# A depthwise convolution on TensorE: 31 taps over 128 channels, or 9 lags over 4 time phases x 32 channels

## The chip, the cores and the metric

The kernel runs on all 8 cores of one Trainium2 chip. Every core runs the same program on one of the 8 sequences of the batch; the cores exchange nothing. The metric is the device time in microseconds (us) of the slowest core.

## The reference

Two layers over x of shape (8, 2048, 1024). What a layer computes:

```python
h = rmsnorm(x, g_mix)
zq, zf, zi, zog, zglu, zga, zgb = split(h @ w_in)
o = hgrn2_recurrence(silu(zq), 1 - f, zi, log f)        # 4 heads of 128, chunked gated linear recurrence
y_a = (rmsnorm(o) * silu(zog)) @ w_br_a
u = (zglu[:, :512] + b) * sigmoid(zglu[:, 512:] + b)    # GLU, 512 channels
u = causal_dwconv(u, conv_w, conv_b)                    # 31 taps, each channel by itself
y_b = silu(layernorm(u)) @ w_br_b                       # LayerNorm over the 512 channels
x = x + (sigmoid(zga) * y_a + sigmoid(zgb) * y_b) @ w_out
x = x + conv_ffn(rmsnorm(x)); x = x + sigmoid(rmsnorm(x) @ w_ple_gate) * (p @ w_ple_proj)
```

The change touches only the branch with `u`: the GLU's output, the depthwise convolution, the LayerNorm behind it, and the order of the work that surrounds them.

## The kernel before, in words

Channels lie on partitions and time along the free dimension. A sequence is worked in two halves of T = 1024 frames (`hf`), so `mixer` (L468) is called four times: two layers, two halves. One call goes through these stages, each of them a list of instructions in a fixed order for each engine; there is no scheduler on the chip, and an engine takes its instructions in order. Every operation goes through one of the helpers `mm` (L266), `act` (L275), `tt` (L279), `stt` (L283), `ts` (L288 or L291), `cp` (L295), so the profile's lines are those of the helpers; waits on semaphores come from the tiles that an operation reads and writes.

- Gates: projections for q, f, v and the output gate (`gate_ph1`, `gate_ph2`). They end in Ln and Exp on ScalarE and a scan on VectorE.
- `fill_steps` (L569), a generator, and `rec_steps` (L627), another, are woven into one another (L694 to L702). `fill_steps` first makes the GLU: for each of 4 blocks of 128 channels and each of 2 time tiles of 512, 8 matmuls for the gate half and 8 for the value half, a sigmoid, and a `stt` into `u[cc]`. Then comes the convolution: for each block `cc` and time tile, 31 matmuls of 512 columns accumulate in one PSUM bank; tap k's stationary matrix is 128x128 with the tap's 128 weights on its diagonal, its moving operand is `u[cc]` shifted by k. The 124 diagonal matrices are made by VectorE for every call (`build_dg`, L565: identity times a column of weights). An activation adds the bias and writes `uc32[cc]` in float32. That makes 48 steps, 16 of the GLU and 32 of the convolution.
- `rec_steps` is the recurrence over 8 chunks of 128 frames in 34 steps: `keys` (4 transposes, 8 score matmuls, masks), `outer` (4 matmuls, the state's update on VectorE, its copy on ScalarE), `rows` (8 matmuls, a square, a product), `scale` (1 matmul with ones, Ln, Exp, a product). Banks 0 to 4 of PSUM belong to it, one for each kind of result; banks 5 to 7 to `fill_steps`. After step i of `fill_steps`, the steps of the recurrence are emitted until `done * 48 >= (i + 1) * 34`.
- LayerNorm (L705 to L737): casts and squares of `uc32` by time tile, 16 matmuls with a matrix of ones that sum over the channels, then for each time tile mean and variance, Ln, Exp, and for each block subtract, multiply, Silu into `ucs[cc]`.
- Branches (L739 to L776): for each of 8 output blocks, 16 matmuls for gate A (`pA`), 8 for branch A (`pC`), a sigmoid and a product, then 16 for gate B (`pB`) and 8 for branch B (`pD`, which read `ucs`), a sigmoid, a product and a sum into `y[oc]`. `ps2()` hands out four pairs of PSUM banks in turn.
- The output projection, woven with the next norm.

Weights come in blocks of up to 1 MB through five SBUF slots: `wrel` frees a block and issues the next load on the POOL queue (`w_emit_upto`). The SP queue loads x at the start and stores the output at the end, and is idle in between.

Of the kernel before, what the change touches and what calls it, by code (L numbers as in the profile page):

```python
# [18 lines left out]
NCOL = 368  # L19
C_GMIX, C_GFFN, C_GPLE, C_GFIN, C_HGN, C_BGLU, C_CW, C_CB, C_LNG, C_LNB, C_FW, C_FB, C_LG0, C_LG1 = (  # L20
    0, 8, 16, 24, 32, 33, 41, 165, 169, 173, 177, 309, 353, 357)
NCONST = 128 + 128 + 512
# [1010 lines left out]
```

How the kernel before makes its waits and increments, by code:

```python
    def _wait(self, eng, deps):  # L70
        for k, v in deps.items():
            if self.seen[eng].get(k, 0) >= v:
                continue
            self.seen[eng][k] = v
            sem = self.sem[k] if isinstance(k, str) else k
            self.q[eng].append(lambda e, sem=sem, v=v: e.wait_ge(sem, v))
# [22 lines left out]
    def op(self, eng, fn, reads=(), writes=(), inc=True):  # L99
        self._wait(eng, self._deps(eng, reads, writes))
        if inc:
            self.cnt[eng] += 1
            c = self.cnt[eng]
            sem = self.sem[eng]
            self.q[eng].append(lambda e, fn=fn, sem=sem: fn(e).then_inc(sem, 1))
        else:
            c = self.cnt[eng] + 1
            self.q[eng].append(fn)
        for t in _flat(reads):
            if t.r.get(eng, 0) < c:
                t.r[eng] = c
        for t in _flat(writes):
            t.w = (eng, c)
            t.r = {}
# [1 line left out]
    def dma(self, eng, fn, out_t=None, in_t=None, sem_t=None):  # L116
        reads = [in_t] if in_t is not None else []
        writes = [out_t] if out_t is not None else []
        self._wait(eng, self._deps(eng, reads, writes))
        st = out_t if out_t is not None else sem_t
        if st.dsem is None:
            st.dsem = self.new_sem()
        st.dcnt += 16
        sem, v = st.dsem, st.dcnt
        self.q[eng].append(lambda e, fn=fn, sem=sem: fn(e).then_inc(sem, 16))
        if out_t is not None:
            out_t.w = (sem, v)
            out_t.r = {}
        if in_t is not None:
            in_t.r[sem] = v
```

## Time and profile before

| | |
|---|---|
| runs, us | 2771.02, 2443.6, 2827.24 (median 2771.02) |
| the profiled execution | 2442.08 us; span of its slowest core 2440.5 us |
| spans of the 8 cores | 2420.8 to 2440.5 us, mean granted TensorE clock 0.969 to 0.975 |
| PE busy | 2246.7 us (92%), 10528 matmuls |
| VectorE (DVE) busy | 1436.5 us (59%), 2357 instructions |
| ScalarE (ACT) busy | 1125.6 us (46%), 1442 instructions |
| DMA queue of POOL (q0), of SP (q1) | 140.55 MB and 39.3%, 17.49 MB and 2.4% of 16 engines' span |

The profile is one execution, on the slowest core. Its parts are the busy times, the span in 40 slices, the DMA queues, the chain of waits that ended last, the costliest groups of instructions, and the DMA issues. A PE that shows as busy is not at its peak, because the durations of pipelined matmuls overlap: the distance from one start to the next is what a matmul costs.

### The profile page before, as it was taken

How to read it: one execution, taken by the hardware profiler on the slowest of the kernel's cores; microseconds unless marked ns; L12 is line 12 of the kernel's file. 1: busy time of each engine (PE TensorE's matmuls, PEld its weight loads, DVE VectorE, ACT ScalarE, POOL GpSimd, SP SyncE). 2: the span in 40 equal slices, each digit the busy share in tenths (PEclk: the TensorE clock that was granted, in tenths of full speed). 3: DMA queues.
4: the chain of work that ended last, by engine and by line, in shares of the span. 5: the costliest groups of instructions: out<-in, count | busy, mean ns of one | idle time of the engine just before them, and what ended most of it. 6: DMA issues, size and time to landing. Idle time of an engine off the chain costs nothing.

```text
span 2440.5 us, 30096 instructions; the slowest of 8 cores (2420.8 to 2440.5 us)
## 1 busy us (share of the span) xinstructions
PE 2246.7 (92%) x10528; PEld 1018.0 (42%) x10528; DVE 1436.5 (59%) x2357; ACT 1125.6 (46%) x1442; POOL 146.8 (6%) x169
## 2 busy tenths in 40 slices
PE   3898898988999999999888989989899999999985
PEld 1344343443444444444334433445334444444432
DVE  3665356753589538943666553666437982697256
ACT  2644235442277507752445343453425771576144
POOL 0000000000000100010000000000000010001000
PEclk9999999999999999999999999989999999999998
DMA  9430352403443555364434206242064454546533
GB/s 199 85 57 1 52 76 42 74 1 52 70 77 56 67 86 86 47 89 73 63 50 71 34 9 95 35 70 35 9 95 69 61 68 67 90 63 84 75 48 138
DMA packets 175523, 159.96 MB, mean 66 GB/s; under 512 B 3856, under 2 KB 166032, under 8 KB 175376
## 3 DMA queue, kind: packets, MB, share of 16 engines
q0 software_dynamic: 165584, 140.55, 39.3%
q1 hardware_dynamic: 9792, 17.49, 2.4%
q8 instruction: 87, 1.43, 0.2%
q14 instruction: 60, 0.49, 0.1%
HBM read 290.18 MB, written 8.39 MB: 122 GB/s over the span
## 4 chain that ended last, share of the span: by engine, by line
PE 81%; DVE 8%; ACT 4%; DMA 4%; issue 3%; SPq 1%; DVEq 0%; another core or an unknown queue 0%; ACTq 0%; POOLq 0%
PE ps L266 80%; DVE arena L279 4%; ACT arena L275 3%; DVE arena L283 2%; DMA ws_sb<-w_br_b 1%; DMA ws_sb<-w_br_a 1%; ACT L275 1%; DMA x_sb<-xT 1%; SPq L386 1%; DMA outT<-arena 1%; DVE h_sb L283 0%; DVE arena L528 0%; DVE x_sb L279 0%; PE ps L634 0%; DVE arena L288 0%
## 5 line engine op out<-in xcount | busy, mean ns | idle before, releaser
L266 PE MATMUL ps<-h_sb,ws_sb 128*128 128x512 bf16 x5376 | 1219.4, 386 | 61.3 <-DVE arena L283 24.1
L266 PEld LDWEIGHTS ps<-h_sb,ws_sb 128*128 128x128 bf16 x5376 | 529.3, 99 | 713.8 <-issue 109.1
L275 ACT ACTIVATE arena<-ps 128x1024 bf16<-128x1024 f32 (+4 forms) x500 | 405.4, 830 | 737.9 <-PE ps L266 735.9
L266 PE MATMUL ps<-arena,ws_sb 128*128 128x512 bf16 x2816 | 649.3, 388 | 56.1 <-DVE arena L279 32.5
L283 DVE SCALAR_TENSOR_TENSOR arena<-arena,cv_sb 128x1024 f32<-128x1024 bf16 x352 | 432.4, 1280 | 43.0 <-ACT arena L275 41.5
L266 PEld LDWEIGHTS ps<-arena,ws_sb 128*128 128x128 bf16 x2816 | 278.5, 99 | 409.2 <-issue 93.7
L279 DVE TENSOR_TENSOR arena<-arena 128x1024 bf16<-128x1024 f32 (+2 forms) x288 | 257.0, 910 | 109.5 <-ACT arena L275 103.6
L266 PE MATMUL ps<-arena 128*128 128x512 bf16 (+3 forms) x1632 | 285.6, 315 | 12.0 <-ACT arena L275 8.5
L279 DVE TENSOR_TENSOR arena<-arena,ps 128x1024 f32<-128x1024 f32 x96 | 116.8, 1220 | 282.1 <-PE ps L266 219.6
L275 ACT ACTIVATE arena<-arena 128x512 f32<-128x512 f32 (+2 forms) x308 | 223.0, 747 | 121.6 <-DVE arena L279 78.6
L275 ACT ACTIVATE arena<-ps,cv_sb 128x1024 f32<-128x1024 f32 (+1 forms) x240 | 255.0, 1062 | 37.5 <-PE ps L266 33.5
L279 DVE TENSOR_TENSOR x_sb<-ps,x_sb 128x1024 f32<-128x1024 f32 x64 | 78.3, 1224 | 282.7 <-PE ps L266 282.7
L266 PEld LDWEIGHTS ps<-arena 128*128 128x128 bf16 (+1 forms) x1632 | 144.6, 98 | 145.2 <-issue 15.3
L275 ACT ACT_TABLE_LOAD x96 | 123.2, 1283 | 161.0 <-PE ps L266 142.5
L275 ACT ACTIVATE arena<-x_sb 128x512 bf16<-128x512 f32 x216 | 115.8, 617 | 114.9 <-PE ps L266 76.0
L266 PE MATMUL ps<-arena,ones 128*128 128x512 bf16 x320 | 89.5, 394 | 46.6 <-ACT arena L275 21.1
L283 DVE SCALAR_TENSOR_TENSOR h_sb<-x_sb,cv_sb,arena 128x512 bf16<-128x512 f32 x160 | 109.0, 746 | 0.0
L288 DVE TENSOR_SCALAR arena<-ident,cv_sb 128x128 bf16<-128x128 bf16 x496 | 85.3, 253 | 3.5 <-PE ps L266 3.5
L283 DVE SCALAR_TENSOR_TENSOR arena<-ps,cv_sb,arena 128x512 f32<-128x512 f32 (+1 forms) x64 | 47.7, 745 | 57.0 <-ACT arena L275 45.6
L327 POOL DMA_DIRECT2D ws_sb<-w_up x48 | 42.0, 876 | 618.4 <-PE ps L266 618.4
L266 PEld LDWEIGHTS ps<-arena,ones 128*128 128x128 bf16 x320 | 31.6, 99 | 96.2 <-issue 66.1
L327 POOL DMA_DIRECT2D ws_sb<-w_in x40 | 35.1, 882 | 555.8 <-PE ps L266 553.6
(49 smaller groups left out, 583.5 us busy)
## 6 DMA issues: line engine op xcount, KB each, us to landing
ws_sb<-w_in POOLq DMA_DIRECT2D x40, 1024.0 KB, 13.5
ws_sb<-w_up POOLq DMA_DIRECT2D x40, 1024.0 KB, 10.2
ws_sb<-w_down POOLq DMA_DIRECT2D x32, 704.0 KB, 7.4
x_sb<-xT SPq DMA_DIRECT2D x32, 256.0 KB, 16.6
ws_sb<-w_out POOLq DMA_DIRECT2D x8, 1024.0 KB, 14.4
ws_sb<-w_ple_gate POOLq DMA_DIRECT2D x8, 1024.0 KB, 10.2
outT<-arena SPq DMA_DIRECT2D x32, 256.0 KB, 2.3
ws_sb<-w_br_a POOLq DMA_DIRECT2D x8, 512.0 KB, 12.7
```

The source lines that it names most:

```text
L266: P.op("pe", lambda e: e.matmul(out_ap, l_ap, r_ap, start=start, stop=stop), reads=[l_t, r_t], writes=[out_t], inc=inc)
L275: P.op("act", lambda e: e.activation(out=out_ap, in_=in_ap, func=func, **kw), reads=[in_t] + list(rd), writes=[out_t])
L279: P.op(eng, lambda e: e.tensor_tensor(out=out_ap, in0=a_ap, in1=b_ap, op=op), reads=[a_t, b_t], writes=[out_t])
L283: P.op("dve", lambda e: e.scalar_tensor_tensor(out=out_ap, in0=a_ap, scalar=scalar, in1=b_ap, op0=op0, op1=op1), reads=[a_t, b_t] + list(r ...
L288: P.op(eng, lambda e: e.tensor_scalar(out=out_ap, in0=a_ap, scalar1=s1, scalar2=None, op0=op0), reads=[a_t] + list(rd), writes=[out_t])
L327: return e.dma_start(out=sap[:, 0:k * ncol].rearrange("p (k n) -> p k n", k=k), in_=src[l, :, c0:c0 + ncol].rearrange("(k p) n -> p k n", ...
L386: P.dma("sp", lambda e, kc=kc: e.dma_start(out=xt[kc][hf][t_].ap, in_=xT[kc * 128:(kc + 1) * 128, c0:c0 + 512]), out_t=xt[kc][hf][t_])
```

## The change

The convolution is laid out anew. T = 1024 frames are split into 4 phases (frame t = 4 tau + f) of 256 frames each, and a tile holds 4 phases x 32 channels on its 128 partitions: there are 16 such groups (`NG`) in place of 4 blocks of 128 channels. Output phase b at tau is a sum over input phases a and lags m = 0 to 8 with weight w[30 - (4m + b - a)], so a group takes 9 matmuls of 256 columns, whose 128x128 stationary matrices have four times four blocks of 32x32, each diagonal. VectorE builds the 9 matrices of a group in one product of broadcast operands (`build_dg(g)`), from a table that the host lays out (`cwv`). Four groups' matrices are kept (`NDG`).

- The GLU's `stt` writes `us[cc % 2]` phase by phase (a permuted write); then 16 DMAs on the SP queue (`to_phases`), each 32 partitions x 256 frames in bfloat16, move it to `uP[cc]`. Two `us` tiles take turns.
- Each group's output gets its bias in an activation of 256 columns.
- The sums of the LayerNorm move into `fill_steps` as four steps of their own, 8 matmuls of 256 columns each, with a block matrix of ones (`ones4`) that sums the 32 channels of each phase.
- `ln_apply(cc)`: subtract and multiply over 1024 columns, four Silu of 256 columns, and 16 DMAs on the SP queue that move the result to 128 channels on partitions, with time still ordered by phase; branch B's last product reads PSUM in permuted order.
- The weave has 28 steps in place of 48, and the recurrence starts after the fourth (`lead`).
- Branches, first half: `ln_apply` and branch A in turn for `oi` = 0 to 3, then branch B for `oi` = 0 to 3; second half: A and B in turn. Each `ln_apply(oi)` is emitted ahead of branch A's sigmoid.
- At the start, four small loads more on the POOL queue.

```diff
+    def dmas(self, eng, fns, out_t, in_t):
+        self._wait(eng, self._deps(eng, [in_t], [out_t]))
...
+        for fn in fns:
+            out_t.dcnt += 16
+            self.q[eng].append(lambda e, fn=fn, sem=sem: fn(e).then_inc(sem, 16))
...
-            def build_dg(tiles, cc, part):
-                for k in range(part * 8, min(part * 8 + 8, 31)):
-                    ts(tiles[k], tiles[k].ap, ident, ident.ap, cvl.ap[:, C_CW + cc * 31 + k:C_CW + cc * 31 + k + 1], None, ALU.mult, rd=[cvl])
+            def build_dg(g):
+                d = dgP[g % NDG]
+                tt(d, d.ap.rearrange("p (m c) -> p m c", c=32), i32, i32.ap.unsqueeze(1).to_broadcast([128, NLAG * PH, 32]),
+                   cwv[l], cwv[l].ap[:, g, :].unsqueeze(2).to_broadcast([128, NLAG * PH, 32]), ALU.mult)
+
+            def to_phases(cc):
+                s_ = us[cc % 2].ap.rearrange("p (f t) -> p f t", f=PH)
+                fns = []
+                for q_ in range(4):
+                    for f_ in range(PH):
+                        fns.append(lambda e, q_=q_, f_=f_: e.dma_start(out=uPv[cc][32 * f_:32 * f_ + 32, q_, HALO:UW],
+                                                                      in_=s_[32 * q_:32 * q_ + 32, f_, :]))
+                P.dmas("sp", fns, uP[cc], us[cc % 2])
...
+                        stt(us[cc % 2], usv[:, :, t_ * 128:(t_ + 1) * 128].rearrange("p f t -> p t f"),
+                            pa, pa.ap.rearrange("p (t f) -> p t f", f=PH), cvl.ap[:, C_BGLU + cc:C_BGLU + cc + 1],
+                            sg, sg.ap.rearrange("p (t f) -> p t f", f=PH), ALU.add, ALU.mult, rd=[cvl])
                         if cc >= 2:
-                            build_dg(dg[0][1], 0, (cc - 2) * 2 + t_)
+                            build_dg((cc - 2) * 2 + t_)
                         yield
+                    to_phases(cc)
...
-                        for k in range(31):
-                            tk = dg[cc % 2][1][k]
-                            mm(pc, pc.ap, tk, tk.ap, u[cc], u[cc].ap[:, t_ * 512 + k:t_ * 512 + k + 512], k == 0, k == 30, k == 30)
+                for g2 in range(NG // 2):
...
+                        for m in range(NLAG):
+                            mm(pc, pc.ap[:, j * TAU:(j + 1) * TAU], d, d.ap[:, m * 128:(m + 1) * 128],
+                               uP[cc], uPv[cc][:, q_, HALO - m:HALO - m + TAU], m == 0, m == NLAG - 1, m == NLAG - 1)
+                        act(uc32[cc], uc32[cc].ap[:, q_ * TAU:(q_ + 1) * TAU], pc, pc.ap[:, j * TAU:(j + 1) * TAU], AF.Identity,
+                            bias=cvl.ap[:, C_CB + g:C_CB + g + 1], rd=[cvl])
+                        if g + NDG < NG:
+                            build_dg(g + NDG)
...
+                    for src_, dst_ in ((ucb[cc % 2], p1), (sqb[cc % 2], p2)):
+                        for q_ in range(4):
+                            mm(dst_, dst_.ap[:, 0:TAU], ones4, ones4.ap, src_, src_.ap[:, q_ * TAU:(q_ + 1) * TAU],
+                               cc == 0 and q_ == 0, cc == 3 and q_ == 3, q_ == 3)
...
             n_side = 34
-            n_main = 48
+            n_main = 28
+            lead = 4
             done = 0
             for i, _ in enumerate(fill_steps()):
-                while done * n_main < (i + 1) * n_side:
+                while done * (n_main - lead) < (i + 1 - lead) * n_side:
...
+            def ln_apply(cc):
+                mt, vt = lnst["mt"], lnst["vt"]
+                v3 = uc32[cc].ap.rearrange("p (q t) -> p q t", q=4)
+                tt(uc32[cc], v3, uc32[cc], v3, mt, mt.ap.unsqueeze(1).to_broadcast([128, 4, TAU]), ALU.subtract)
+                tt(uc32[cc], v3, uc32[cc], v3, vt, vt.ap.unsqueeze(1).to_broadcast([128, 4, TAU]), ALU.mult)
+                for q_ in range(4):
+                    g = 4 * cc + q_
+                    act(un[cc], un[cc].ap[:, q_ * TAU:(q_ + 1) * TAU], uc32[cc], v3[:, q_, :], AF.Silu,
+                        bias=cvl.ap[:, C_LNB + g:C_LNB + g + 1], scale=cvl.ap[:, C_LNG + g:C_LNG + g + 1], rd=[cvl])
...
+                P.dmas("sp", fns, ucs[cc], un[cc])
...
+            y = [None] * 8
+            for oi in range(4):
+                ln_apply(oi)
+                branch_a(0, oi)
+            for oi in range(4):
+                branch_b(0, oi)
...
+            for oi in range(4):
+                branch_a(1, oi)
+                branch_b(1, oi)
```

## Rows read from the trace of the kernel before

**Rows 1.** The page's chain of waits that ended last: shares by engine.

```profile
PE 81%; DVE 8%; ACT 4%; DMA 4%; issue 3%; SPq 1%; DVEq 0%; another core or an unknown queue 0%; ACTq 0%; POOLq 0%
```

**Rows 2.** Windows: from the GLU's start to the LayerNorm's sums, all four calls.

Columns: the stretch and its length, then for each engine the busy time and its instructions, then the granted clock, the DMA engines' share and GB/s.

```profile
107.10:227.90 120.80, 109.34 (x592) 54.03 (x593) 72.35 (x222) 53.07 (x86) 3.25 (x4) 0.94 0.34 49
416.50:533.30 116.80, 107.57 (x592) 53.15 (x592) 72.27 (x218) 53.01 (x86) 3.25 (x4) 0.94 0.36 53
1292.00:1408.70 116.70, 105.61 (x592) 52.84 (x593) 72.35 (x222) 52.95 (x86) 3.25 (x4) 0.97 0.34 53
1597.70:1714.50 116.80, 107.56 (x594) 53.26 (x594) 72.27 (x218) 53.05 (x86) 3.25 (x4) 0.94 0.33 52
```

**Rows 3.** Windows of the second call: GLU, convolution, sums, first output block.

```profile
416.50:463.30 46.80, 39.73 (x214) 19.71 (x214) 28.96 (x65) 25.45 (x40) 1.49 (x2) 0.85 0.59 85
463.30:529.30 66.00, 63.88 (x363) 31.96 (x363) 41.14 (x149) 23.56 (x40) 1.76 (x2) 1.00 0.22 33
529.30:533.30 4.00, 3.97 (x16) 1.48 (x16) 2.17 (x7) 4.00 (x8) 0.00 (x0) 1.00 0.01 2
533.30:555.50 22.20, 13.27 (x49) 4.93 (x49) 13.10 (x20) 15.68 (x20) 0.00 (x0) 0.84 0.00 1
```

**Rows 4.** Timeline of PE, second call, in the GLU.

Columns: start, length in us, engine, line, operation, count, and in brackets the idle time before it and what ended it.

```profile
423.08 3.57 PE L266 MATMUL ps<-h_sb,ws_sb 128*128 128x512 bf16 x8 [6.59 <-ACT hsm L275]
...
446.97 0.39 PE L634 MATMUL ps<-ident,arena 128*128 128x128 bf16 x4
447.19 1.19 PE L266 MATMUL ps<-arena 128*128 128x64 bf16 x8
448.31 1.90 PE L266 MATMUL ps<-h_sb,ws_sb 128*128 128x512 bf16 x8
450.05 0.61 PE L266 MATMUL ps<-arena 128*128 128x128 bf16 x8
450.50 3.62 PE L266 MATMUL ps<-h_sb,ws_sb 128*128 128x512 bf16 x16
453.95 0.39 PE L266 MATMUL ps<-arena 128*128 128x128 bf16 x4
```

**Rows 5.** Groups of instructions by form: busy us, mean ns.

```profile
L266 PE MATMUL ps<-arena 128*128 128x512 bf16 x992 | 228.4, 379 | 3.5 <-DVE arena L283 3.5
...
L275 ACT ACTIVATE arena<-ps 128x1024 f32<-128x1024 f32 x96 | 97.8, 1023 | 329.5 <-PE ps L266 329.3
...
L288 DVE TENSOR_SCALAR arena<-ident,cv_sb 128x128 bf16<-128x128 bf16 x496 | 85.3, 253 | 3.5 <-PE ps L266 3.5
...
L279 DVE TENSOR_TENSOR arena<-arena 128x512 f32<-128x512 f32 x72 | 47.6, 688 | 29.3 <-ACT arena L275 26.8
...
L343 POOL DMA_DIRECT2D ws_sb<-w_down x32 | 34.1, 1067 | 325.5 <-PE ps L266 325.5
...
L275 ACT ACTIVATE arena<-arena,cv_sb 128x512 bf16<-128x512 f32 x32 | 25.2, 810 | 4.8 <-DVE arena L279 4.7
...
L279 DVE TENSOR_TENSOR arena<-ps,mask 128x256 bf16<-128x256 f32 x32 | 13.4, 418 | 7.0 <-PE ps L266 7.0
...
L295 DVE CAST arena<-arena 128x512 bf16<-128x512 f32 x32 | 11.1, 421 | 0.0
```

**Rows 6.** Timeline of ACT, second call: the LayerNorm's Silu of the first time tile.

```profile
537.31 1.28 ACT L275 ACT_TABLE_LOAD   x1 [0.87 <-DVE arena L279]
538.61 2.33 ACT L275 ACTIVATE arena<-arena,cv_sb 128x512 bf16<-128x512 f32 x3
```

**Rows 7.** The SP queue's stores of the output: issue, and time to landing.

```profile
L946 SPq DMA_DIRECT2D outT<-arena x32: 332/332/344, 2397.6 to 2438.1; - x32
...
DMA to landing us min/median/max: 2.2/2.3/4.1
```

**Rows 8.** The SP queue's loads of x, beside weight loads.

```profile
L386 SPq DMA_DIRECT2D x_sb<-xT x32: 328/684/4388, 2.9 to 59.6; - x32
...
DMA to landing us min/median/max: 7.3/16.6/23.1
```

More of the change, by code:

```diff
@@ L18 @@
 DFF = 2816
[L19 to L22, printed above, removed]
+PH = 4
+NG = 16
+NLAG = 9
+TAU = T // PH
+HALO = NLAG - 1
+NCOL = 280
+C_GMIX, C_GFFN, C_GPLE, C_GFIN, C_HGN, C_BGLU, C_CB, C_LNG, C_LNB, C_FW, C_FB, C_LG0, C_LG1 = (
+    0, 8, 16, 24, 32, 33, 41, 57, 73, 89, 221, 265, 269)
+NCONST = 128 + 128 + 512 + 32 + 128
 ARENA = 77824
@@ L214, in build_nc @@
         uhalo = Tl(uhalo_sb[:], "uhalo")
+        cwv = [Tl(cwv_sb[:, l], "cwv%d" % l) for l in range(DEPTH)]
+        i32 = Tl(i32_sb[:], "i32")
+        ones4 = Tl(ones4_sb[:], "ones4")
         stash = Tl(stash_sb[:], "stash")
@@ L624, in mixer @@
+                mt, vt = AR(75008, 1024, F32, "mt"), AR(76032, 1024, F32, "vt")
+                act(mt, mt.ap, p1, p1.ap[:, 0:TAU], AF.Identity, scale=1.0 / 512)
+                tt(vt, vt.ap, mt, mt.ap, mt, mt.ap, ALU.mult)
+                stt(vt, vt.ap, p2, p2.ap[:, 0:TAU], 1.0 / 512, vt, vt.ap, ALU.mult, ALU.subtract)
+                act(vt, vt.ap, vt, vt.ap, AF.Ln, bias=EPS)
+                act(vt, vt.ap, vt, vt.ap, AF.Exp, scale=-0.5)
+                lnst["mt"], lnst["vt"] = mt, vt
             p_tr, p_sc, p_kv, p_o, p_ss = bank1[0:5]
@@ L724, in mixer @@
-            for t_ in range(2):
-                sl = slice(t_ * 512, (t_ + 1) * 512)
-                p1, p2 = lnp[t_]
-                mt, vt = mt2[t_], vt2[t_]
-                act(mt, mt.ap, p1, p1.ap, AF.Identity, scale=1.0 / 512)
-                tt(vt, vt.ap, mt, mt.ap, mt, mt.ap, ALU.mult)
-                stt(vt, vt.ap, p2, p2.ap, 1.0 / 512, vt, vt.ap, ALU.mult, ALU.subtract)
-                act(vt, vt.ap, vt, vt.ap, AF.Ln, bias=EPS)
-                act(vt, vt.ap, vt, vt.ap, AF.Exp, scale=-0.5)
-                for cc in range(4):
-                    tt(uc32[cc], uc32[cc].ap[:, sl], uc32[cc], uc32[cc].ap[:, sl], mt, mt.ap, ALU.subtract)
-                    tt(uc32[cc], uc32[cc].ap[:, sl], uc32[cc], uc32[cc].ap[:, sl], vt, vt.ap, ALU.mult)
-                    act(ucs[cc], ucs[cc].ap[:, sl], uc32[cc], uc32[cc].ap[:, sl], AF.Silu,
-                        bias=cvl.ap[:, C_LNB + cc:C_LNB + cc + 1], scale=cvl.ap[:, C_LNG + cc:C_LNG + cc + 1], rd=[cvl])
@@ L995, in _cvec, with _cwv @@
     return cv
+def _cwv(inp):
+    w = np.asarray(inp["conv_w"], np.float32)
+    out = np.zeros((DEPTH, PH, 32, NG, NLAG, PH), np.float32)
+    for m in range(NLAG):
+        for a in range(PH):
+            for b in range(PH):
+                d = PH * m + b - a
+                if 0 <= d <= 30:
+                    out[:, a, :, :, m, b] = w[:, 30 - d, :].reshape(DEPTH, NG, 32).transpose(0, 2, 1)
+    return out.reshape(DEPTH, 128, NG * NLAG * PH)
 def _consts():
@@ L1005, in _consts @@
     c[:, 256:768] = sm
+    c[:, 768:800] = np.tile(np.eye(32, dtype=np.float32), (PH, 1))
+    c[:, 800:928] = np.kron(np.eye(PH, dtype=np.float32), np.ones((32, 32), np.float32))
     return c
```

208 lines of the change are left out of this document (108 added, 100 removed).

## The prediction, written before the result was known

> **What bounds the kernel now.** I read the chain of waits first: TensorE holds 81% of it [rows 1], so an edit is worth what it does to TensorE's time, once that time isn't replaced by waits. Then I took the windows between the GLU's start and the LayerNorm's sums, for all four calls of `mixer` [rows 2]: 120.8, 116.8, 116.7 and 116.8 us, with VectorE busy for only 72 of them. The split of the second call [rows 3] shows three different stretches. In the GLU (46.8 us) TensorE waits and runs at a clock of 0.85. In the convolution (66.0 us) it is busy for 63.9 us at full clock, with 363 matmuls: nothing but TensorE bounds it. In the first output block (22.2 us) it has 48 matmuls, 10.4 us of work, and waits 12 us for the LayerNorm.
>
> Unit costs come from distances between starts [rows 4]: 8 matmuls of 512 columns take 450.05 - 448.31 = 1.74 us, so 0.216 us each. Eight of 128 columns take 0.45 us, 0.056 each. The 256-column matmul of the change isn't in the trace; by these two it takes 0.108. A chunk of the recurrence costs TensorE 0.22 + 1.12 (`keys`) + 0.45 (`rows`) + about 0.22 (`outer`, four of 128 columns) + 0.22 (`scale`) = 2.2 us. On VectorE it costs five operations of 0.69 and two masks of 0.42 [rows 5], 4.3 us.
>
> **GLU stretch.** Its 256 matmuls take 16 x 1.73 = 27.6 us as before. The opening wait of 6.5 us for `glub` and the cold start behind it (8 matmuls in 3.57 us, not 1.74) stay [rows 4]: the slot is freed and filled as before; I keep 3.5 us for the cold clock. With `lead` the recurrence starts at the fifth step and makes 17 steps (by the weave's condition) by the end, not 11: five `keys`, five `outer`, four `rows`, three `scale`, 10.3 us. ScalarE gets tight, with five operations of 0.6 us a chunk, two table loads of 1.28 around each Ln (the load: [rows 6]) and 1.4 sigmoids of 0.7, 6.5 us against TensorE's 7.1. I add 4 us of waits. Sum 6.5 + 27.6 + 3.5 + 10.3 + 4 = 51.9 us, against 46.8.
>
> The permuted `stt` has as many elements as before; no row shows a permuted write. Its bounds are none and twice 0.75 us, 6 us a call on VectorE, which has 17 us idle here [rows 3]; I take none. `to_phases` adds 16 DMAs a tile on SP, which is otherwise idle. An issue takes 0.332 us and a landing 2.3 [rows 7]: 5.3 + 2.3 = 7.6 us. Behind a tile's DMAs waits the `stt` that writes the same `us` two blocks later, some 13 us on (a block is 6.9 us of GLU plus about 3 of recurrence). So it is covered, and by twice the issue price just so. The fourth tile is read only after 12 groups.
>
> **Convolution and sums.** TensorE now needs 144 x 0.108 = 15.6 us, was 248 x 0.216 = 53.6. Here the bound moves to VectorE. A build is 1152 elements with two tensor operands; from 256 to 512 columns a `tensor_tensor` grows from 418 to 688 ns [rows 5], 1.05 ns an element, so a build takes 0.418 + 896 x 0.00105 = 1.36 us alone and about 1.23 in a row. The bound below is a rate twice that, 0.65 us, which the bfloat16 builds of before suggest (253 ns for 128 elements, 85.3/496 = 0.172 in a row). I take 1.23, since the nearest rows in kind are those of `tensor_tensor`. The first six steps of the convolution carry 12 builds (14.8 us) and nine recurrence steps (9.1 us): 23.9 us of VectorE against 108 x 0.108 + 4.7 = 16.4 us of TensorE. With 1.6 us of waits inside the recurrence and 2 us for the last two steps, whose builds are done by then, the convolution takes 27.5 us. Then the four LayerNorm steps: ScalarE has four squares of 1.05, two Ln-Exp pairs, a copy and a square, 7.8 us, and the state's update goes ahead of the first cast, so 9.5 us. Sum 37 us, against 66 + 4 = 70.0 [rows 3].
>
> Casts, halo copies and bias activations are hidden: the same columns, and 8 more fixed costs of 0.2 us on a ScalarE that isn't the bound there. That cover goes only if ScalarE were full.
>
> The Trainium skill, VectorE: DVE Perf Modes, Mode 2x_1P, wants 16-bit elements with a step of one in both operands for two results a cycle. The weight operand here has step zero, so by that page the build stays at the slow rate; no row here shows a product of two bfloat16 tensors, and the sum would be the same.
>
> So from GLU to sums 88.9 us, was 116.8: 27.9 us less in three calls. The first call's opening wait is 4.3 us, not 6.5 (the same view of TensorE), so 86.7 against 120.8, 34.1 less. Together 117.8 us less.
>
> **LayerNorm and first output block.** Here it pays back. The engines' orders couple three things: VectorE takes subtract, multiply (1.22 each), then `t1s`, which waits for the sigmoid; ScalarE takes a table load 1.28, four Silu of 256 columns (0.81 for 512 [rows 5], so about 0.56 each in a row), another load 1.28, the sigmoid 1.02; the next `ln_apply` starts behind `t1s`. One round is 2.44 + 1.28 + 2.24 + 1.28 + 1.02 + 1.22 + 0.2 = 9.7 us, where TensorE's branch A has 24 x 0.216 = 5.2. From the last recurrence matmul, statistics and the first multiply take 5.6 us, the first Silu set 3.5 more, three rounds 29: the last `un` is whole at 38 us. Its 16 DMAs end 7.6 us later, at 45.7. No weight load runs then (DMA share 0.00 [rows 3]). Only now can the first `pD` run: 1.7 us, plus 3.4 for a cold clock after a wait of over 10 us, 50.8. By then TensorE has 120 matmuls behind it. Before, that point was at 22.2 + 72 x 0.216 = 37.8. So 13 us more a call, 52 in all. The wait for `br1` in the second half (issued after the same release) and what follows don't change. The four start-up loads, 0.7 us of POOL issue each, go behind the first four blocks: nothing.
>
> **Sum.** -117.8 + 52 = -66, against the profiled execution's 2442.08: **2376 us**. The median of the three runs shown is 2771, 13% above it, the lowest 2443.6: the forecast is for an execution like the profiled one.
>
> **Rivals.**
>
> The DMAs decide (slower). The Trainium skill, DMA: Bandwidth & Descriptors, Rules for kernel authors, says that transfers under 64 KB are mostly overhead and should be joined; these are 16 KB. In rows: SP's loads of x took 0.684 us at the median and landed after 16.6 beside weight loads [rows 8], and POOL's costliest issue is 1.07 [rows 5]. At 0.684 the queue falls behind in the first output block, 9.1 + 64 x 0.684 + 2.3 = 55.2 against 45.7: +38 us, 2414. At 1.07 it ends at 79.9, +34 a call, and in the GLU each tile takes 17 us, so that `us` and the last blocks wait some 20 more: +54 x 4, 2592, slower. It turns at 0.8 us an issue, where the two extras make 17 us a call. For it: nothing in the trace moves 32 partitions. Against: 32 stores went at 0.332 without exception. By the fixed 2.0 us of that page's Anatomy of one DMA, taken one after another, it would be slower still.
>
> The recurrence has a floor of its own (no change). Now chunks go by every 12 us, hidden by matmuls. My forecast wants 7 to 9. Transpose, copy, scores, mask, rows, square, Ln, Exp and product are each a hop between engines; if a chunk can't go under 10 us, GLU to sums stays at 101 instead of 88.9: +48, 2424. For it: PE waits for ScalarE at the first chunks. Against: VectorE and ScalarE have 18 and 21 us idle in the GLU [rows 3].
>
> Cheap builds (faster). At 0.65 us TensorE bounds the convolution again, 7 us less a call: 2348.
>
> The gain isn't there at all: if a 256-column matmul cost 0.14 us (what the 64-column ones cost, 1.12/8 [rows 4]), TensorE would need 4.6 us a call more, mostly under VectorE: +8. That stays inside the range.
>
> **Chances.** Forecast 0.52, cheap builds 0.10, recurrence floor 0.25, DMA 0.13 (0.10 of it beyond 2491). Two per cent, 49 us, is what a measurement of this kernel tells from no change: 2393 and 2491. Of the forecast's own case 0.04 lies above 2393. Faster 0.48 + 0.10 = 0.58, same 0.04 + 0.25 + 0.03 = 0.32, slower 0.10. The range goes from 2335 (cheap builds and 3 us less waiting a call) to 2440 (the floor, with some of the DMA's price).
>
> **What would show it.** Right: conv matmuls at 0.108; builds near 1.3 us; GLU to sums 85 to 93 us with VectorE over 80% busy in the convolution; eight table loads in each first half of the branches; TensorE waiting over 8 us ahead of the first `pD`, released by a DMA into `ucs`; SP issues of 0.33. Wrong: `stt` of the GLU waiting for the SP queue, chunks at a pace over 9 us, or a first output half no longer than before.

## The result: 5% slower

The kernel after the change takes 2571.56 us (median of four executions, 2564.91 to 2661.25), against 2607.31 for the four of the kernel before that were run beside it (2442.49 to 2827.24). The ratio is 1.052, 95% interval 1.046 to 1.058: slower. (In some executions of every kernel one die runs at a lower clock and ends later; the ratios leave these out, and where e3 is spoken of as 2467 us, that is the longest span of its undisturbed die.) The profiled execution took 2564.91 us, its span 2563.4, against 2442.08 and 2440.5. The forecast was 2376.

The page of the kernel after: busy time by engine, then the chain of waits that ended last.

```profile
PE 2183.7 (85%) x10176; PEld 1019.1 (40%) x10176; DVE 1480.4 (58%) x1869; ACT 1168.5 (46%) x1502; POOL 148.9 (6%) x173
...
PEclk9977899868999999999998689987789999999998
...
PE 68%; DVE 12%; ACT 9%; issue 6%; SPq 2%; DMA 2%; DVEq 0%; ACTq 0%; another core or an unknown queue 0%
```

TensorE has 63 us less to do and its share of the chain falls from 81% [rows 1] to 68%; VectorE, ScalarE and the issue of instructions take its place. The clock row has sixes and sevens where the mixer's four calls lie. The windows say where the time went: GLU's start to the end of the sums, all four calls, the columns as in [rows 2].

```profile
108.00:244.19 136.19, 90.52 (x505) 53.02 (x505) 85.34 (x109) 56.40 (x89) 3.25 (x4) 0.74 0.37 53
444.90:579.89 134.99, 88.22 (x505) 52.16 (x505) 85.17 (x105) 56.63 (x90) 3.25 (x4) 0.75 0.35 54
1348.90:1487.75 138.85, 93.35 (x505) 54.19 (x505) 85.33 (x109) 56.38 (x89) 3.25 (x4) 0.72 0.34 51
1688.10:1826.91 138.81, 93.19 (x505) 54.39 (x505) 85.33 (x105) 56.65 (x90) 3.25 (x4) 0.71 0.34 51
```

These are 548.8 us, where [rows 2] add up to 471.1: +77.7, forecast -117.8. The rest of the span is 45.2 us longer (122.9 in all), forecast +52. So nearly the whole error lies in this stretch. Split as in [rows 3], second call:

```profile
444.90:508.60 63.70, 45.66 (x244) 22.75 (x243) 46.44 (x60) 32.08 (x49) 1.49 (x2) 0.84 0.50 76
508.60:562.70 54.10, 33.75 (x222) 23.65 (x219) 32.84 (x37) 18.86 (x36) 1.75 (x2) 0.72 0.30 45
562.70:579.89 17.19, 8.80 (x42) 5.76 (x43) 5.89 (x9) 5.69 (x8) 0.00 (x0) 0.55 0.00 0
579.89:634.09 54.20, 31.27 (x121) 12.50 (x120) 15.77 (x15) 27.21 (x34) 1.49 (x2) 0.81 0.22 39
```

GLU 63.7 (forecast 51.9), convolution 54.1 (27.5), sums 17.2 (9.5). The last row is A0 to A3 with B0, 54.2 (50.8). No engine is full in any of them, so this is a matter of waits. TensorE's timeline, second call (columns as in [rows 4]):

```profile
485.42 0.38 PE L290 MATMUL ps<-arena 128*128 128x128 bf16 x4 [2.66 <-ACT arena L299]
485.63 3.25 PE L290 MATMUL ps<-h_sb,ws_sb 128*128 128x512 bf16 x8
...
508.38 1.47 PE L290 MATMUL ps<-arena 128*128 128x128 bf16 x13
518.46 2.08 PE L290 MATMUL ps<-arena 128*128 128x256 bf16 x9 [8.61 <-ACT arena L299]
...
538.28 2.08 PE L290 MATMUL ps<-arena 128*128 128x256 bf16 x9 [4.67 <-ACT arena L299]
...
552.75 1.15 PE L290 MATMUL ps<-arena 128*128 128x256 bf16 x9 [2.62 <-ACT arena L299]
...
565.78 2.29 PE L290 MATMUL ps<-arena,ones 128*128 128x256 bf16 x9 [3.47 <-DVE arena L319]
...
621.92 0.38 PE L290 MATMUL ps<-arena,ws_sb 128*128 128x512 bf16 x1 [3.58 <-DMA arena<-arena]
632.01 2.29 PE L290 MATMUL ps<-arena,ws_sb 128*128 128x512 bf16 x5 [9.71 <-DMA arena<-arena]
```

Nine matmuls of a group take 1.15 us at full clock, the next start 0.98 later, 0.109 each as forecast (552.75). Behind the waits of 8.61 and 4.67 us they take 2.08, at the lower of the clock's two levels (granted 0.50 in both stretches). The wait of 8.61 us stands in front of the second group of a pair. What it waited for, on ScalarE and on VectorE:

```profile
510.02 0.59 ACT L299 ACTIVATE arena<-ps 128x512 bf16<-128x512 f32 x1
517.33 0.63 ACT L299 ACTIVATE arena<-arena 128x512 bf16<-128x512 f32 x1 [6.71 <-DVE arena L303]
517.86 0.46 ACT L299 ACTIVATE arena<-ps,cv_sb 128x256 f32<-128x256 f32 x1
```

```profile
510.71 3.15 DVE L307 SCALAR_TENSOR_TENSOR arena<-ps,cv_sb,arena 128x512 f32<-128x512 f32 x2 [1.39 <-ACT arena L299]
513.47 1.57 DVE L303 TENSOR_TENSOR arena<-i,cwv_sb 128x1152 bf16<-128x1152 bf16 x1
514.96 0.68 DVE L303 TENSOR_TENSOR arena<-ps,S 128x512 f32<-128x512 f32 x1
515.74 1.49 DVE L303 TENSOR_TENSOR arena<-arena,hsm 128x512 f32<-128x512 f32 x2
```

All waits of 0.7 to 8.6 us in this convolution stand ahead of the second group of a pair. The two groups share one PSUM bank, which is one tile to the kernel's dependency tracking. The second group writes that tile, so it must wait until the bias activation of the first has read it; that activation (517.86) stands behind the recurrence's copy (517.33), and the copy behind VectorE's queue of products and a build.

By form, the changed instructions:

```profile
L307 DVE SCALAR_TENSOR_TENSOR arena<-ps,cv_sb,arena 128x512 bf16<-128x512 f32 x32 | 79.6, 2489 | 8.3 <-PE ps L290 4.1 <-ACT arena L299 3.8
L303 DVE TENSOR_TENSOR arena<-i,cwv_sb 128x1152 bf16<-128x1152 bf16 x64 | 90.2, 1409 | 34.0 <-PE ps L290 34.0
L290 PE MATMUL ps<-arena 128*128 128x256 bf16 x576 | 112.8, 365 | 79.9 <-ACT arena L299 79.9
L299 ACT ACT_TABLE_LOAD x120 | 154.0, 1283 | 202.5 <-PE ps L290 142.3 <-DVE arena L303 54.8 <-DMA cv_sb<-cvec 3.7
```

The permuted `stt` takes 2.49 us (0.75 taken, 1.5 the upper bound). All of the 79.9 us of idle time ahead of the convolution's matmuls, four calls together, is put down to ScalarE; e1 tests that it comes by way of the bank. In the SP queue's issues (ns min/median/max) the sixteens of the two layout moves cost 0.575 us each, not 0.33 [rows 7]:

```profile
L597 SPq DMA_DIRECT2D arena<-arena x256: 507/575/1803, 128.2 to 1766.3; - x128
L767 SPq DMA_DIRECT2D arena<-arena x256: 507/575/1090, 254.3 to 1877.5; - x128
```

### The profile page after: what moved, and what is told of

Its sections match the earlier page's. It is cut to its first block, busy times and chain, and to the rows that moved or that the text cites. A ratio compares the mean times of both kernels' runs of the same rounds, so it can differ in the third digit from the quotient of the medians.

```text
span 2563.4 us, 29529 instructions; the slowest of 8 cores (2544.6 to 2563.4 us)
## 1 busy us (share of the span) xinstructions
PE 2183.7 (85%) x10176; PEld 1019.1 (40%) x10176; DVE 1480.4 (58%) x1869; ACT 1168.5 (46%) x1502; POOL 148.9 (6%) x173
## 4 chain that ended last, share of the span: by engine, by line
PE 68%; DVE 12%; ACT 9%; issue 6%; SPq 2%; DMA 2%; DVEq 0%; ACTq 0%; another core or an unknown queue 0%
PE ps L290 68%; ACT arena L299 6%; DVE arena L303 6%; DVE arena L307 3%; ACT L299 3%; SPq L767 1%; DVE S L303 1%; DMA x_sb<-xT 1%; DVE arena L552 1%; SPq L410 1%; DMA outT<-arena 1%; DVE h_sb L307 0%; DVE arena L319 0%; DVE x_sb L303 0%; PE ps L679 0%
## 5 line engine op out<-in xcount | busy, mean ns | idle before, releaser
L290 PE MATMUL ps<-h_sb,ws_sb 128*128 128x512 bf16 x5376 | 1237.7, 390 | 72.8 <-ACT arena L299 38.2
L299 ACT ACTIVATE arena<-ps 128x1024 bf16<-128x1024 f32 (+5 forms) x496 | 402.7, 831 | 705.7 <-PE ps L290 702.0
L303 DVE TENSOR_TENSOR arena<-arena,ps 128x1024 f32<-128x1024 f32 x96 | 117.0, 1219 | 346.9 <-PE ps L290 208.3
L299 ACT ACTIVATE arena<-ps,cv_sb 128x1024 f32<-128x1024 f32 (+2 forms) x272 | 263.1, 968 | 117.1 <-PE ps L290 110.5
L303 DVE TENSOR_TENSOR arena<-arena 128x1024 bf16<-128x1024 f32 (+3 forms) x252 | 249.6, 1004 | 78.2 <-ACT arena L299 72.7
L290 PE MATMUL ps<-arena 128*128 128x256 bf16 (+2 forms) x1216 | 188.2, 302 | 124.3 <-ACT arena L299 113.4
L290 PEld LDWEIGHTS ps<-arena 128*128 128x128 bf16 x1216 | 128.6, 120 | 184.2 <-issue 145.3
L299 ACT ACTIVATE arena<-x_sb 128x512 bf16<-128x512 f32 x216 | 115.8, 618 | 116.8 <-PE ps L290 71.6
L290 PE MATMUL ps<-arena,ones 128*128 128x512 bf16 (+1 forms) x384 | 103.1, 411 | 76.7 <-DVE arena L319 34.7
L307 DVE SCALAR_TENSOR_TENSOR arena<-ps,cv_sb,arena 128x512 bf16<-128x512 f32 (+1 forms) x64 | 102.9, 1619 | 60.2 <-ACT arena L299 55.5
L303 DVE TENSOR_TENSOR arena<-i,cwv_sb 128x1152 bf16<-128x1152 bf16 x64 | 90.2, 1409 | 34.0 <-PE ps L290 34.0
L290 PEld LDWEIGHTS ps<-arena,ones 128*128 128x128 bf16 x384 | 42.9, 114 | 124.6 <-issue 94.9
## 6 DMA issues: line engine op xcount, KB each, us to landing
ws_sb<-w_ple_gate POOLq DMA_DIRECT2D x8, 1024.0 KB, 11.4
```

The costliest lines, as they stand in the source:

```text
L290: P.op("pe", lambda e: e.matmul(out_ap, l_ap, r_ap, start=start, stop=stop), reads=[l_t, r_t], writes=[out_t], inc=inc)
L299: P.op("act", lambda e: e.activation(out=out_ap, in_=in_ap, func=func, **kw), reads=[in_t] + list(rd), writes=[out_t])
L303: P.op(eng, lambda e: e.tensor_tensor(out=out_ap, in0=a_ap, in1=b_ap, op=op), reads=[a_t, b_t], writes=[out_t])
L307: P.op("dve", lambda e: e.scalar_tensor_tensor(out=out_ap, in0=a_ap, scalar=scalar, in1=b_ap, op0=op0, op1=op1), reads=[a_t, b_t] + list(r ...
```

## The experiments

Times are medians; ratios are to the kernel before, with their 95% intervals.

### Taking the waits out of the convolution

**e1_bank**: the eighteen matmuls of both groups ahead of both activations.

```diff
+                    for j in range(2):
+                        g = 2 * g2 + j
+                        q_ = g % 4
```

> The changed kernel with one edit: both groups of a PSUM bank are multiplied before either is read, so the second group's first matmul no longer waits for the activation that reads the first. Theory A (coupling: the stretch from GLU to sums grew because TensorE waits behind reads of a bank it still writes, and behind VectorE's slow permuted write): the waits of 8.6, 4.7 and 2.6 us and some of 0.7 in the convolution go, of about 19 us a call a part comes back as other waits; 10 to 15 us less a call, 2505 to 2525 us. Theory B (the recurrence's own chain of hops sets the pace): under 5 us a call, 2545 us or more.

2509.34 us, 1.028 (1.026 to 1.030): 56 us less than the profiled execution of after, 14 a call, as expected. No wait in the convolution is over 4 us any more. In their place come short ones, on the builds now, such as:

```profile
498.31 3.23 PE L290 MATMUL ps<-arena 128*128 128x256 bf16 x18 [1.98 <-DVE arena L303]
```

**e2_stt**: the same elements in the other loop order; writes run on, reads step by four.

```diff
-                        stt(us[cc % 2], usv[...].rearrange("p f t -> p t f"), pa, pa.ap.rearrange("p (t f) -> p t f", f=PH), ...
+                        stt(us[cc % 2], usv[...], pa, pa.ap.rearrange("p (t f) -> p f t", f=PH), ...
```

> The changed kernel with one edit: the GLU's product runs through its elements phase by phase, so it writes contiguously and reads its two inputs with a step of four; the values are the same. Theory A: it takes about 0.75 us in place of 2.49, VectorE has 14 us less in the GLU of a call, and the waits of TensorE for ScalarE and VectorE there shrink: 8 to 14 us less a call, 2510 to 2535 us. Theory B: VectorE's load isn't what sets the pace, 2550 or more. If the strided reads are as dear as the strided write, the duration stays near 2.5 us and nothing moves.

2544.71 us, 1.042 (1.040 to 1.045): by the measure of e1, 5 us a call (20.2 in all). That lies between the two theories; the instruction goes to 1.12 us, not to 0.75:

```profile
L307 DVE SCALAR_TENSOR_TENSOR arena<-ps,cv_sb,arena 128x512 bf16<-128x512 f32 x32 | 35.8, 1120 | 6.6 <-ACT arena L299 4.6 <-PE ps L290 1.6
```

By the Trainium skill, VectorE: DVE Perf Modes, Mode 1×, the fallback mode works with any stride and gives one result a cycle; then the order of the loops would be free. The runs differ: in this instruction steps cost on both sides (1.12 us) and most on the write side (2.49, against 0.75 in order).

**e3_both**: both edits.

> Both edits of the two runs before. Theory A: GLU to sums falls from 135 us to 105 to 112, time 2450 to 2485 us. Theory B: it stays above 120 us, 2510 or more. Neither edit touches the first output block, which keeps its 54 us.

2486.58 us, 1.018 (1.016 to 1.019). It wins 24 us a call on after by the 2467 us (20 by the median) and is still no faster than the kernel before. GLU to sums, second call (112.4 to 113.3 us on the eight cores):

```profile
421.13:533.74 112.61, 79.46 (x499) 48.56 (x505) 73.86 (x105) 55.70 (x90) 3.26 (x4) 0.82 0.44 65
```

**e4_lead0**: e3 with `lead = 0`.

> The kernel of the third run (both edits: contiguous write, both groups of a bank multiplied before it is read; 2486.6 us) with lead = 0: the recurrence starts at the first step of the weave and its 34 steps spread over all 28. Theory A (the stretch is bound by hops between engines that the weave leaves uncovered, and fewer steps of the recurrence per unit of TensorE work are what costs): 1 chunk less per stretch hardly changes that; the wait of 5 us at the first chunk, seen in the kernel before, returns and 3 to 5 us at the end go: 2475 to 2500. Theory B (the late start of the recurrence is what made the stretch long): 5 us a call or more, below 2466.

2463.41 us, 1.008 (1.006 to 1.010). The number lies in theory B's range, but the profiled spans reach 2458.2, only 9 less than 2467: 2.2 us a call, the small gain of theory A.

### Is a cheap convolution worth what it saves?

**e5_9taps**: the kernel before with 9 of the 31 taps computed and the rest left out, `n_main = 32`. Its TensorE work falls about as the change meant it to, with neither layout nor transfers.

```diff
-                        for k in range(31):
+                        for k in range(9):
...
-            n_main = 48
+            n_main = 32
```

> The kernel before with 9 of the 31 taps computed (the rest of the convolution is left out, its diagonal matrices too) and the weave set for 32 steps: 38 us less of TensorE and 15 us less of VectorE a call, in the old layout, without any transfer. Theory A: the old weave turns most of it into time, GLU to sums 80 to 90 us in place of 117, 2300 to 2340 us. Theory B (a floor of about 10 us a chunk): GLU to sums stays at 100 us or more, 2375 or more.

2351.87 us, 0.963 (0.961 to 0.964). In between the two theories: 38 us of TensorE a call leave, and the stretch goes from 116.8 to 95.9.

```profile
390.40:486.30 95.90, 73.56 (x418) 36.99 (x418) 59.07 (x133) 55.43 (x89) 3.25 (x4) 0.88 0.44 64
```

So even without the new layout 17 of 38 us come back as waits. The first and last `keys` transposes of its eight chunks start at 399.77 and 466.50: 9.5 us a chunk in the mean, where it was 11.4 before (426.45 and 506.53). That mean is no floor of a chunk. Between 419.24 and 428.39 TensorE doesn't wait at all: four times eight matmuls of the GLU and a chunk's own 2.2 us make these 9.15 us. The last period in the convolution takes 6.6 us:

```profile
459.88 0.63 PE L634 MATMUL ps<-ident,arena 128*128 128x128 bf16 x4
...
466.50 0.39 PE L634 MATMUL ps<-ident,arena 128*128 128x128 bf16 x4
```

### The first output block

**e6_split**: e3 with every second DMA of `ln_apply` on POOL's queue.

```diff
-                P.dmas("sp", fns, ucs[cc], un[cc])
+                P.dmas("sp", fns[0::2], ucs[cc], un[cc])
+                P.dmas("pool", fns[1::2], ucp[cc], un[cc])
```

> The kernel of the third run with the 16 transfers of each ln_apply issued in turn by the SP and the POOL queue, 8 each. Theory A (the issue time of 0.575 us behind the last tile is on the path): the last tile's issue shrinks from 9.2 to some 5 us, the wait of 9 us ahead of the first product with ucs by about 4.4: 2465 to 2473. Theory B (the DMA engines or the landing set that wait): no change, 2482 or more.

2457.61 us, 1.006 (1.003 to 1.009); the profiled die 0 ends at 2447.2, 20 less than 2467, the gain that was expected. POOL issues one in 0.496 us.

**e7_lnfirst**: e6 with the four `ln_apply` in front of branch A. **e9_nosplit**: the same without e6's split.

```diff
             for oi in range(4):
                 ln_apply(oi)
+            for oi in range(4):
                 branch_a(0, oi)
```

> As the run before, and all four ln_apply are emitted ahead of the first branch A. Theory A (the round VectorE - Silu - table load - sigmoid - VectorE, 10.3 us long and gone through four times, makes the first output half late): un is complete at about 18 us in place of 40, one table load to Silu and one back in place of eight, the first pD at about 34 in place of 45 to 50: 16 to 18 us less a call than the third run, 2415 to 2425. Theory B (the transfers set the end of that stretch): they end hardly earlier, 2460 or more.

> All four ln_apply ahead of branch A, but their 64 transfers on the SP queue alone. Theory A (two bounds lie close together in the first output half: the coupled rounds, and 64 issues of 0.575 us on one queue; the run with tanh shortened the rounds to 7.6 us and won nothing): the queue ends at 9.6 + 64 x 0.575 + 1.8 = 48 us after the sums, no earlier than with the rounds: 2455 to 2475, as the third run. Theory B (the order alone is worth the 55 us that order and split won together): 2420 or less.

e7 takes 2403.05 us, 0.985 (0.983 to 0.986), the profiled spans up to 2400.7: 17 us a call less than e3. Its first output block (A0 to A3 with B0) takes 37.3 us, where the same 120 matmuls took 37.8 before. One wait is left in it:

```profile
534.97 5.24 PE L290 MATMUL ps<-h_sb,ws_sb 128*128 128x512 bf16 x16 [9.61 <-ACT arena L299]
```

e9 takes 2475.01, 1.013 (1.008 to 1.017), profiled spans up to 2467.8, level with e3: nothing won, as its theory A had it. The same order is worth 46 us with two queues (2447.2 to 2400.7) and none with one. TensorE and SP in e9:

```profile
576.87 0.58 PE L290 MATMUL ps<-arena,ws_sb 128*128 128x512 bf16 x1 [7.59 <-DMA arena<-arena]
585.59 2.29 PE L290 MATMUL ps<-arena,ws_sb 128*128 128x512 bf16 x5 [8.13 <-DMA arena<-arena]
```

```profile
543.26 41.02 SPq L770 DMA_DIRECT2D arena<-arena  x64
```

64 issues take 41.0 us one after another, 0.64 us each in the mean.

**e8_tanh**: e3 with the sigmoids of the branches as tanh, whose table Silu shares.

```diff
-                act(s_, s_.ap, pA, pA.ap, AF.Sigmoid)
-                tt(t1s[oi], t1s[oi].ap, s_, s_.ap, pC, pC.ap, ALU.mult)
+                act(s_, s_.ap, pA, pA.ap, AF.Tanh, scale=0.5)
+                stt(t1s[oi], t1s[oi].ap, s_, s_.ap, 1.0, pC, pC.ap, ALU.add, ALU.mult)
```

> The kernel of the third run with the gates' sigmoid computed as 0.5 * (tanh(x / 2) + 1): Tanh shares a table with Silu in the trace (the gates' six activations run behind one load), the factor 0.5 is taken in the residual's update, and the number of instructions is unchanged. Theory A: eight table loads of 1.28 us go from each first half, a round falls from 10.3 to 7.7 us, 8 to 9 us less a call: 2450 to 2456. Theory B (the loads hide behind other waits): 2478 or more.

A miss: 2468.98 us, 1.011 (1.010 to 1.013), level with e3's 2467. The rounds did shorten, from 10.3 to 7.6 us; the time went into waits for the same queue:

```profile
576.27 0.59 PE L290 MATMUL ps<-arena,ws_sb 128*128 128x512 bf16 x1 [7.84 <-DMA arena<-arena]
586.20 2.29 PE L290 MATMUL ps<-arena,ws_sb 128*128 128x512 bf16 x5 [9.34 <-DMA arena<-arena]
```

```profile
544.64 40.23 SPq L770 DMA_DIRECT2D arena<-arena  x64
```

So two bounds of nearly the same length lie over one another here: the rounds of ScalarE and VectorE, and the SP queue. Taking away one bares the other: the order alone is worth nothing (e9), the shorter rounds alone nothing (e8), the split alone 20 us (e6), order and split together 66 (2467 to 2400.7).

### What holds the stretch from GLU to sums

**e10_f**: e7 with `lead = 0`. **e12_nobuild**: e10_f with the 12 later builds of a call left out (later groups use old matrices).

> The run with all ln_apply first and split queues (2403 us), and lead = 0. Theory A (lead = 0 wins some 3 us a call between GLU and sums, and what it showed beyond that was a disturbed die of the run it was compared with): 2385 to 2397. Theory B (it wins the full 23 us): 2375 to 2382.

> The second kernel of this call with 12 of the 16 builds of stationary matrices left out in every call (the first four groups' matrices are used again). Theory A (VectorE's builds bound the convolution): the convolution shrinks from 37 us to the 22 to 28 that TensorE needs with its share of the recurrence, 8 us or more a call, 2360 or less. Theory B (the recurrence's hops set the pace, the builds fill gaps): 3 us a call at most, 2378 or more.

e10_f: 2408.81 us in the median, 0.985 (0.968 to 1.001), profiled spans 2380.8 to 2393.8: 7 us less than e7 in all, if anything. e12: 0.968 (0.963 to 0.972), spans 2350.3 to 2365.6. That is 28 us, 7 a call, between its two theories: of the 16.2 us of VectorE that the 12 builds take, not half lies on the path.

**e13_norec**: e10_f with the recurrence's 34 steps left out of the weave.

```diff
-                while done * (n_main - lead) < (i + 1 - lead) * n_side:
-                    next(rec, None)
-                    done += 1
-            for _ in rec:
```

> e10_f with the recurrence's 34 steps left out of the weave (its outputs are not made; everything else stands). In e10_f GLU to sums takes 102 us in the second call, of which the recurrence's own TensorE work is 8 chunks of about 2.2 us, 18 us. Theory A: what stretches this stage is that the recurrence's chains of hops between engines and the fill share the engines' orders. Then the stage falls by well over its own 18 us, to 57 to 65 us (16 GLU tiles of 1.73 and a cold clock, 31 us; 7.5 us of opening wait; 144 matmuls of 0.108 with builds on VectorE 16 to 20; sums 6), 37 to 45 us a call: 2205 to 2240 against 2385 to 2394. Theory B: builds, transfers and evictions of the fill itself set the pace. Then it falls by only about 18 us, to 84, and the time to 2310 to 2320.

2233.07 us, 0.914 (0.912 to 0.916). Windows of e10_f and of e13, GLU to sums, second call:

```profile
399.60:508.86 109.26, 80.05 (x505) 48.34 (x505) 73.77 (x105) 55.19 (x89) 3.25 (x4) 0.84 0.44 66
```

```profile
365.70:438.20 72.50, 54.04 (x305) 31.52 (x305) 42.05 (x50) 26.39 (x45) 3.25 (x4) 0.88 0.66 100
```

And TensorE in the convolution and the sums of e13:

```profile
408.63 9.71 PE L290 MATMUL ps<-arena 128*128 128x256 bf16 x72 [4.24 <-DVE arena L307]
421.63 5.76 PE L290 MATMUL ps<-arena 128*128 128x256 bf16 x36 [3.29 <-DMA arena<-arena]
...
432.48 0.60 PE L290 MATMUL ps<-arena,ones 128*128 128x256 bf16 x4
...
438.20 3.62 PE L290 MATMUL ps<-h_sb,ws_sb 128*128 128x512 bf16 x16
```

36.8 us a call leave, of which the recurrence's own TensorE work is 8 x 2.2 = 17.6: the recurrence costs at least 19.2 us a call beyond its matmuls. The time was as theory A had it; the stage, put at 57 to 65 with its opening wait (the 102 us beside it are e10_f's without), is 72.5. What makes it longer is a queue that lay hidden before. The SP queue issues the 64 moves of the four tiles without a break, and the GLU's product waits for it, twice:

```profile
383.79 43.30 SPq L597 DMA_DIRECT2D arena<-arena  x64
```

```profile
396.07 1.11 DVE L307 SCALAR_TENSOR_TENSOR arena<-ps,cv_sb,arena 128x512 bf16<-128x512 f32 x1 [5.45 <-DMA arena<-arena]
...
407.27 1.11 DVE L307 SCALAR_TENSOR_TENSOR arena<-ps,cv_sb,arena 128x512 bf16<-128x512 f32 x1 [6.53 <-DMA arena<-arena]
```

TensorE's waits for these two products and for the moves themselves come to 9.9 us (1.17 at 397.32, 4.24, 3.29, and 1.15 at 428.54). In e10_f nothing waits for this queue. So without it the fill would need less than 72.5, and the recurrence's 19.2 is a lower bound. No run took both away.

### Can it be had back?

**e11_best**: e10_f with tanh as in e8 and the order `ln_apply` 0 and 1, A0, 2, A1, 3, A2, A3.

> Split queues, lead = 0, gates by tanh, and the order ln_apply 0, 1, A0, ln_apply 2, A1, ln_apply 3, A2, A3: with no table loads between Silu and Tanh, TensorE's idle time of 9.6 us after A1 shrinks to about 3 and one of about 3 arises ahead of the first product with ucs. 3 to 5 us a call less than the run before: 2368 to 2382. If the transfers are behind again, it equals the run before.

2380.86 us, 0.975 (0.970 to 0.980), in the range expected: faster than both kernels, by 2.5% and 7%. The first output block takes 35.3 us, with four waits of 0.6 to 2.3 us in it. The gates by tanh could be had in the kernel before as well; that wasn't run, so how much of the 2.5% is owed to the new layout is open.

**e14_pool**: e11 with every second one of the 12 later builds on POOL.

```diff
-                   cwv[l], cwv[l].ap[:, g, :].unsqueeze(2).to_broadcast([128, NLAG * PH, 32]), ALU.mult)
+                   cwv[l], cwv[l].ap[:, g, :].unsqueeze(2).to_broadcast([128, NLAG * PH, 32]), ALU.mult,
+                   eng="pool" if g >= NDG and g % 2 else "dve")
```

> e11_best with every second of the 12 later builds of a group's matrices moved from VectorE to POOL, which is idle but for weight loads. Theory A: leaving out 12 builds won 7 us a call, so moving 6 of them wins up to half, 3.5 us a call, 14 in all: 2355 to 2370 against 2367 to 2385. Theory B: POOL is slower at a product of two 16-bit tensors, or takes VectorE's share of SBUF: a build there takes over 3 us, it comes late for its group, and nothing is won or time is lost: 2380 and above.

2390.61 us, 0.978 (0.977 to 0.980), as theory B had it; the intervals overlap, and nothing is won. First POOL, then VectorE, second call:

```profile
476.12 2.12 POOL L303 TENSOR_TENSOR arena<-i,cwv_sb 128x1152 bf16<-128x1152 bf16 x1 [6.07 <-PE ps L290]
479.14 2.42 POOL L303 TENSOR_TENSOR arena<-i,cwv_sb 128x1152 bf16<-128x1152 bf16 x1 [0.90 <-PE ps L290]
```

```profile
474.34 1.34 DVE L303 TENSOR_TENSOR arena<-i,cwv_sb 128x1152 bf16<-128x1152 bf16 x1
...
479.50 3.27 DVE L303 TENSOR_TENSOR arena<-i,cwv_sb 128x1152 bf16<-128x1152 bf16 x1
```

Alone a build takes VectorE 1.34 us. The one that starts at 479.50, while POOL's of 479.14 runs until 481.56, takes 3.27: 2.06 of waiting and 1.21 of work. The Trainium skill, SBUF — State Buffer, Who interferes with whom, says that a VectorE instruction with two SBUF inputs and a GpSimd one that reads SBUF exclude each other for the whole instruction; this trace agrees.

## Why the prediction was wrong, step by step

**What failed is "the convolution takes 27.5 us"**, and with it "GLU stretch ... Sum 51.9" and "9.5 us" for the sums: 88.9 together against 135.0 (+26.6, +11.8 and +7.7). The convolution's term was made as VectorE's load plus 3.6 us of waits, as if work on one engine only had to fit beside that of the other. "Slower" had a chance of 0.10, all of it for the rival with the DMAs, and it wasn't they that made the kernel slower.

The missing 46.1 us of the second call divide, by windows of the runs, into 22.4 for bank and write (135.0 to e3's 112.6), 3.3 for the later start of the recurrence (to e10_f's 109.3; the times of e3 and e4 give 2.2), 11.8 for the recurrence and 8.6 for the fill. The last two come so: without what it gives to the recurrence, the sum has 6.5 + 27.6 + 3.5 for the GLU, 14.8 + 2 for the convolution and 9.5 for the sums, 63.9 us, where e13 has 72.5; and it gives the recurrence 25.0 (17.6 of matmuls and 7.4 of waits and VectorE's load), where e13 takes away 36.8.

- **A wait that the sum doesn't have, 14 us** (e1, by that edit alone). The diff showed it: the `mm` and the `act` of each group use `pc`, and there is one `pc` for two groups. The step costed the activations as "hidden", by their duration; what counts is that the next matmuls wait for their end, behind whatever stands ahead of them on ScalarE. The prediction's own part on added waits should have asked that.
- **The permuted write, 5 us alone** (e2), about 8 on top of the bank (22.4 less 14). The bounds were none and twice 0.75; it is 3.3 times, outside of them, and no row had stood behind the factor of two.
- **The recurrence, at least 19.2 us beyond its 17.6 of TensorE** (e13), where the sum had 7.4. In the kernel before, 53.6 us of convolution lay between its hops. Chunks went by every 11.4 us before, 13.5 after (transposes at 462.49 and 557.22), 10.8 in e10_f, 9.5 in e5; the forecast needed 7 to 9. The rival "recurrence floor" was right that the recurrence holds the stretch: the mended versions lie at 109 to 113, where it said 101. But a floor of 10 us a chunk, its mechanism, is not what the runs show: single chunks go by in 6.6 us (e5) and in 7.4 (e10_f, transposes at 450.06 and 457.48). What the recurrence adds shows as single waits. In e10_f TensorE waits 11.1 us ahead of matmuls of the recurrence, all put down to ScalarE, the longest 3.68 and 3.32; another 5.1 in the convolution, put down to VectorE's line of builds and products; and 5.8 for the casts of the sums. Which of these a better order would take away wasn't tested. The 7 us of the builds (e12) may be in part the same waits, since they stand in VectorE's order between the hops.
- **The fill itself, 8.6 us.** "So it is covered" was said of the moves on the SP queue, and in the changed kernel that holds: no `stt` of the GLU waits for SP. In e13 it fails: the queue costs TensorE 9.9 us of waits, with the very sign that the prediction named as one of being wrong. The forecast gave a tile's issues 5.3 us (16 x 0.332); in e13 they take 10.8.
- **The sums, 17.2 us for 9.5.** The last rounds wait 3.5, 3.0 and 2.3 us for a cast, and what follows each runs at the lower clock. In e13 they take 5.7 us (432.48 to 438.20), so this excess comes with the recurrence, whose steps stand among them.
- **The clock.** 3.5 us a call were put in for the cold start. The stretch went at 0.75, against 0.94 before [rows 2]. Behind the waits of 3.0 us and more the matmuls run at 1.2 GHz at first; behind shorter ones some do and some don't (those at 552.75, after 2.62 us, are at full clock). The lower clock came with the waits: e3, with the longest gone, is back at 0.82. No run holds the clock and changes the waits, so its own share is open.

**The first output block was nearly right.** 54.2 us for 50.8, +16.4 a call for +13; rounds of 10.3 for 9.7; the wait for a DMA ahead of `pD` is there, 3.58 and 9.71 for "over 8"; table loads go from 96 to 120, six more a call, eight in each first half. The reason was only half of it: the 64 issues of the queue take 40.6 us (0.575 each at the median, 0.63 in the mean) and are as long as four rounds, so e8 and e9 won nothing. The rival "DMAs decide" put the turn at 0.8 us an issue; that was for the whole kernel to end slower, and at 0.575 the queue decides this block only together with the rounds. The Trainium skill, DMA: Bandwidth & Descriptors, Rules for kernel authors, says that spreading DMAs over queues doesn't add bandwidth and only saves issue time; here issue time was the bound, and e7 against e9 shows what it is worth.

**"The wait for `br1` in the second half doesn't change" was wrong, in the change's favour.** In the first call of the kernel before TensorE waits 4.03 us for `w_br_b` at 288.87, and 4.07, 4.46 and 4.44 in the others; after, no wait for it is left. The longer first block gives that load the time: 16.4 less 4.0 is 12.4 a call, near 50 for four, and 45.2 us outside the stretch were measured.

**Sizes that held:** conv matmuls 0.109 (0.108), builds 1.35 alone (1.36; 1.28 in a row in e13 for 1.23; 1.41 in the mean of after), landing 1.8 (2.3), and the permuted read of PSUM in branch B costs nothing (1219 ns mean for the 96 products of that form, 1220 before).

Still open: what the recurrence's 19.2 us are made of. Neither a recurrence spread over more PSUM banks, nor one with its VectorE work moved, nor e13 with the moves on two queues was run.

## What to carry to other kernels

When a woven side chain of small cross-engine steps hides under long matmuls, much of a saving in those matmuls can come back as waits (17 of 38 us in e5). Two cheap runs help before any layout is written: one with the matmuls left out, one with the chain left out. A mean pace of its chunks doesn't tell it, as the rest of the work is in it. Where two results share a PSUM bank and one tile, the second's first matmul waits for the first's eviction, with all that stands ahead of it on that engine: emit both, then evict. If two bounds of equal length overlap (here the rounds and a DMA queue), removing one shows little or nothing; try both together before either is called free. And a run with a part left out can meet a bound that lay hidden (here the same queue in e13): read its waits before its difference is taken as the part's price.
